# Feed-forward with seven block products in every second pair, two weight block sums made by accumulating transfers

## What is computed

```python
def sq_relu_mlp(h, w1, w2):
    return jnp.square(jax.nn.relu(h @ w1)) @ w2

x = x + g2 * sq_relu_mlp(h2, w1[l], w2[l])   # h2: 256 x 2048, w1: 2048 x 8192, w2: 8192 x 2048
return rmsnorm(x, final_norm_g)
```

## Time and profile before

| | |
|---|---|
| median of 3 runs | 1491.27 us (1491.06 to 1492.92) |
| profiled execution | 1491.33 us, of which the span from first to last instruction is 1489.5 |
| TensorE busy | 1459.4 us (98%), 7252 matmuls; granted clock 0.998 |
| VectorE busy | 1107.0 us (74%) |
| ScalarE busy | 710.5 us (48%) |
| GpSimd busy | 115.0 us (8%) |
| transfers | 355.95 MB, mean 239 GB/s |

### The profile page before, as it was taken

The page is one execution under the profiler, slowest core; times in us unless marked ns, Lnnn a source line. Parts: engine busy times, 40 slices in busy tenths (PEclk is TensorE's granted clock), DMA queues, the critical chain, the costliest instruction groups (busy, mean ns, idle before and its releaser), DMA issues.

```text
span 1489.5 us, 18858 instructions
## 1 busy us (share of the span) xinstructions
PE 1459.4 (98%) x7252; PEld 1201.0 (81%) x7252; DVE 1107.0 (74%) x1342; ACT 710.5 (48%) x996; POOL 115.0 (8%) x92
## 2 busy tenths in 40 slices
PE   5999999999999999999999999999999999999997
PEld 2567888888888888888888888888888888888886
DVE  2456866867667678998777568778757999789976
ACT  3423444565554453334454434434444666456654
POOL 0000000101000000010100000000301322002200
PEclk9999999999999999999999999999999999999999
DMA  9997776764666679889665577787575665656552
GB/s 368 379 361 261 261 253 210 225 201 144 233 216 229 224 226 356 322 295 356 242 223 155 163 264 273 262 306 268 191 235 177 202 216 187 195 183 222 194 197 81
DMA packets 123053, 355.95 MB, mean 239 GB/s; under 512 B 10962, under 2 KB 11986, under 8 KB 122322
## 3 DMA queue, kind: packets, MB, share of 16 engines
q1 hardware_dynamic: 121348, 353.17, 69.7%
q10 hardware_dynamic: 1616, 1.57, 0.3%
HBM read 352.60 MB, written 2.10 MB: 238 GB/s over the span
## 4 chain that ended last, share of the span: by engine, by line
PE 88%; DVE 5%; ACT 2%; issue 2%; DMA 2%; ACTq 0%; POOL 0%; POOLq 0%; DVEq 0%
PE bank L1691 20%; PE bank L1693 20%; PE bank L1692 20%; PE bank L1977 14%; PE bank L1980 7%; PE bank L1847 2%; DVE wl L1202 2%; PE bank L1820 1%; DMA raw<-in_w_ada 1%; ACT wh L748 1%; PE bank L1722 1%; PE bank L1810 1%; DVE acc L1233 1%; DMA ident<-in_identity 1%; PE bank L1773 0%
## 5 line engine op out<-in xcount | busy, mean ns | idle before, releaser
L1202 DVE TENSOR_TENSOR wl<-raw,wh 128x1024 fp32r<-128x1024 f32 x425 | 527.5, 1257 | 227.6 <-ACT wh L748 209.2
L748 ACT ACTIVATE wh<-raw 128x1024 fp32r<-128x1024 f32 x328 | 341.5, 1059 | 296.8 <-PE bank L1980 141.5
L1977 PE MATMUL bank<-h2S,wh 128*128 128x512 f32 x896 | 245.2, 395 | 0.8 <-DVE wl L1202 0.7
L1691 PE MATMUL bank<-wh,hT 128*128 128x512 f32 x512 | 206.8, 404 | 0.5 <-DVE wl L1202 0.5
L1693 PE MATMUL bank<-wh,hT 128*128 128x512 f32 x512 | 200.1, 391 | 0.0
L1692 PE MATMUL bank<-wl,hT 128*128 128x512 f32 x512 | 199.7, 390 | 0.0
L1977 PEld LDWEIGHTS bank<-h2S,wh 128*128 128x128 f32 x896 | 153.1, 189 | 21.9 <-DVE wl L1202 0.9
L1024 ACT ACTIVATE wh<-raw 128x1024 fp32r<-128x1024 f32 (+1 forms) x128 | 125.8, 1002 | 70.3 <-PE bank L1693 64.2
L1233 DVE SCALAR_TENSOR_TENSOR acc<-raw,cc,acc 128x1024 f32<-128x1024 f32 x120 | 153.5, 1279 | 0.0
L1691 PE MATMUL bank<-wh,hidS 128*128 128x512 f32 x392 | 152.6, 389 | 0.3 <-DVE wl L1202 0.3
L1980 PEld LDWEIGHTS bank<-h2S,wl 128*128 128x128 f32 x896 | 137.5, 189 | 19.0
(11 more groups left out here) (253 smaller groups left out, 2075.9 us busy)
## 6 DMA issues: line engine op xcount, KB each, us to landing
raw<-in_w SPq DMA_DIRECT2D x256, 512.0 KB, 4.7
raw<-in_w_ada SPq DMA_DIRECT2D x192, 512.0 KB, 6.0
raw<-in_w_in SPq DMA_DIRECT2D x128, 512.0 KB, 4.6
raw<-in_w_attn_o SPq DMA_DIRECT2D x32, 512.0 KB, 6.4
raw<-in_w_out SPq DMA_DIRECT2D x32, 512.0 KB, 5.8
raw<-in_w_fourier SPq DMA_DIRECT2D x16, 512.0 KB, 6.8
xt<-in_x SPq DMA_DIRECT2D x2, 1024.0 KB, 6.4
ct<-in_ctx SPq DMA_DIRECT2D x2, 1024.0 KB, 11.0
```

The lines of the kernel that those rows point to most:

```text
L748: nc.scalar.activation(slot, raw[:, s % RAW, :], ACT.Copy).then_inc(wh_done, 1)
L1202: nc.vector.tensor_tensor(lo, raw[:, s % RAW, :], hi.bitcast(F32), ALU.subtract)\
L1691: nc.tensor.matmul(bank[b][:], a_hi, w_hi, start=first, stop=False)
L1977: nc.tensor.matmul(out[:], wh[:, slot, cols_f[f]], h2S[:, block, :, :].rearrange("p v t -> p (v t)"), start=(block == 0), stop=False)
```

## The change

Sevens stand in every second pair: 4, 6, ..., 26 of the first block (12) and 5, 7, ..., 25 of the second (11), 23 in place of 15. Two of the four weight sums are no longer made by DVE. SP loads the upper right block of the pair twice into a buffer `tS` (two of them, in turn), and GpSimd issues two transfers that add the upper left and the lower right block to it on the way (accumulating transfers); DVE makes the two other sums, both behind the plain pair. ACT copies the halves of `tH` before the token parts, and `tH` may be overwritten once TensorE's fifth product of the seven before has used it (`t_used`). The combination runs in a buffer `comb` of its own place (over `tL`) and begins two pairs behind the last seven, with its last two steps together.

```diff
-SEVEN_AT = ((3, 6, 9, 12, 15, 18, 21, 24), (5, 8, 11, 14, 17, 20, 23))
+SEVEN_AT = ((4, 6, 8, 10, 12, 14, 16, 18, 20, 22, 24, 26), (5, 7, 9, 11, 13, 15, 17, 19, 21, 23, 25))
...
-COMBINE_AT = {3: ("first", "second"), 4: (0,), 5: (1,), 6: (2,), 7: (3,)}
+COMBINE_AT = {2: ("first", "second"), 3: (0,), 4: (1,), 5: (2, 3)}
...
-PRESCALED_AT = {6: 0, 9: 1, 12: 2, 15: 3}
+PRESCALED_AT = {6: 0, 8: 1, 9: 2, 11: 3}
...
-        tF = place("tF", [P, 4, HC], F32, "h")
+        tF = place("tF", [P, 2, HC], F32, "h", 4096)
...
+        comb = place("comb", [P, 4, HC], F32, "h", 16384)
+        tS = [place("tS0", [P, 2, HC], F32, "h"), place("tS1", [P, 2, HC], F32, "f", 4096)]
...
                 sp.dma_start(raw[:, (S2 + n) % RAW, :], w2[k * P:(k + 1) * P, col * NC:(col + 1) * NC]).then_inc(raw_full[(S2 + n) % RAW], 16)
+                if n % 2 == 0 and n // 2 + 1 in SEVENS[1:]:
+                    i = n // 2 + 1
+                    s = SEVENS.index(i)
+                    c, p = divmod(i, NP)
+                    if s == 1:
+                        sp.wait_ge(hid_ready, 4 + 2 * (N1 - 1))
+                    if s >= 2:
+                        sp.wait_ge(t_lo, 2 * s - 2)
+                        sp.wait_ge(t_sum, s - 1)
+                    for j in range(2):
+                        sp.dma_start(tS[s % 2][:, j, :], w2[2 * p * P:(2 * p + 1) * P, c * NC + HC:(c + 1) * NC]).then_inc(t_first[s % 2], 16)
...
-            for i in SEVENS:
-                _, p, s, _ = PAIRS[i]
-                k1, k2 = 2 * p, 2 * p + 1
+            def token_sums(s):
+                k1, k2 = 2 * PAIRS[SEVENS[s]][1], 2 * PAIRS[SEVENS[s]][1] + 1
                 if s:
                     pool.wait_ge(a_lo, 3 * s)
...
+            def weight_sums(s):
+                c, p, _, _ = PAIRS[SEVENS[s]]
+                row, col = 2 * p * P, c * NC
+                if s == 0:
+                    pool.wait_ge(t_start, 32)
+                else:
+                    pool.wait_ge(t_first[s % 2], 32 * (s // 2 + s % 2))
+                nc.gpsimd.dma_start(tS[s % 2][:, 0, :], w2[row:row + P, col:col + HC], accum_op=ALU.add).then_inc(t_acc[s % 2], 16)
+                nc.gpsimd.dma_start(tS[s % 2][:, 1, :], w2[row + P:row + 2 * P, col + HC:col + NC], accum_op=ALU.add).then_inc(t_acc[s % 2], 16)
+
+            pool.wait_ge(gemm_done, M2)
+            p = SEVENS[0]
+            for j in range(2):
+                nc.gpsimd.dma_start(tS[0][:, j, :], w2[2 * p * P:(2 * p + 1) * P, HC:NC]).then_inc(t_start, 16)
+            pool.wait_ge(hid_ready, 4 + 2 * (N1 - 1))
+            token_sums(0)
+            weight_sums(0)
+            for s in range(1, len(SEVENS)):
+                weight_sums(s)
+                token_sums(s)
...
             def seven_hi(i, p, s):
+                if s:
+                    act.wait_ge(t_used, s)
+                act.wait_ge(t_acc[s % 2], 32 * (s // 2 + 1))
+                nc.scalar.activation(tH[:, 0:2, :], tS[s % 2][:], ACT.Copy).then_inc(t_hi, 1)
+                act.wait_ge(t_sum, s + 1)
+                nc.scalar.activation(tH[:, 2:4, :], tF[:], ACT.Copy).then_inc(t_hi, 1)
+                tile_hi(2 * i, HC)
                 if s == 0:
                     act.wait_ge(row_done, 4)
...
-                for j in range(2):
-                    act.wait_ge(t_sum, 2 * s + j + 1)
-                    nc.scalar.activation(tH[:, 2 * j:2 * j + 2, :], tF[:, 2 * j:2 * j + 2, :], ACT.Copy).then_inc(t_hi, 1)
-                tile_hi(2 * i, HC)
                 tile_hi(2 * i + 1)
...
-                    if following is not None:
-                        block_sums(i + 1, following, e)
...
+                if following is not None:
+                    block_sums(i + 1, following)
+
+            def block_sums(i, s):
+                n2 = 2 * i + 1
+                r2 = raw[:, (S2 + n2) % RAW, :]
+                dve.wait_ge(raw_full[(S2 + n2) % RAW], 16 * ((S2 + n2) // RAW + 1))
+                dve.wait_ge(t_acc[s % 2], 32 * (s // 2 + 1))
+                if s:
+                    dve.wait_ge(t_lo, 2 * s)
+                then(nc.vector.tensor_tensor(tF[:, 0, :], tS[s % 2][:, 0, :], r2[:, HC:NC], ALU.add))
+                nc.vector.tensor_tensor(tF[:, 1, :], tF[:, 0, :], r2[:, 0:HC], ALU.add).then_inc(t_sum, 1)
...
-                direct(1, 6, tH[:, 3, :], tL[:, 3, :])
+                direct(1, 6, tH[:, 3, :], tL[:, 3, :]).then_inc(t_used, 1)
```

## The result

The changed kernel takes 1499.79 us (median, 1499.40 to 1500.33), beside 1491.16 us for the kernel before on the same chip: a ratio of 1.0056, with a 95% interval of 1.0041 to 1.0071. It is slower by more than the 0.2% that can be told. The forecast was 1492.4 with a range of 1486.5 to 1501: the range held the time, but the forecast is 7.4 us too low, and the time lies outside the 1490 to 1495 that it gave itself as its own range.

What follows compares the result with a forecast made beforehand. TensorE was taken as the bound by 1.06 us per three pairs, VectorE after the change. From 1491.33 us, less 5.8, plus 6.8 for VectorE and the tail, plus 0.1 for a restart: 1492.4 us, range 1486.5 to 1501.

Steps and rivals of the forecast that it cites:

- TensorE's saving, 5.8 us: TensorE, whole stage: 24 matmuls fewer save 5.44 us, and the first seven's 0.36 us lateness goes; together 5.8 us.
- VectorE's 10.50 for two pairs: VectorE between sevens: one plain pair and one seven take 10.50 us against TensorE's 10.20, later by 0.30 us.
- The lead of 1.1 us and what is lost behind it: VectorE starts each block 1.1 us ahead; TensorE then loses 2.2 us in the first block, 4.3 in the second.
- Tail, 0.3 us: Behind pair 30: one combination step more, 1.4 us, mostly taken up by idle time; 0.3 us is added.
- The chain of fill and accumulation in the steady state, nothing: Fill, two accumulations and two sums between sevens: 14.3 to 22.8 us of 21.0 available; low half taken, costing nothing.
- rival 2: Fill-and-accumulate chain ends last at ACT's and VectorE's wait for the sums; halfway costs 8.5 us, 1501 us; chance 0.14.
- The first accumulation leaves when the first token sums end: Stage start, GpSimd: first accumulation leaves about 1150, needed some 6 us later; 0 to 1 us, taken as 0.
- The clock: TensorE after a wait: only 0.1 us was added to the forecast for a restart.
- VectorE packs tighter: VectorE between sevens packs a little tighter than 10.50 us, so TensorE stays the bound: 1487.1 us; chance 0.18.
- the transfers don't relieve it: VectorE waits as long as the sums took: 1.20 us back in 21 intervals, 25 us, 1517 us; chance 0.04.
- GpSimd's issues slow it: GpSimd's issue of accumulations slows VectorE, in the middle 0.33 us x 21: 7 us, 1499.4 us; chance 0.12.
- the forecast's own range: The forecast case itself, 1490 to 1495 us from 0.1 us either way in an interval; chance 0.52.

Runs made afterwards that it cites:

- the run with later fills: Changed kernel with a small early GpSimd addition, first accumulations ahead of the token sums, and the second seven's fills one pair later on SP: 1494.28 us, ratio 1.0020.
- the run with the small addition: Changed kernel plus one 128x1 GpSimd addition directly behind its second row sum, order of the stage unchanged: 1498.80 us, ratio 1.0047.
- both edits: Changed kernel with the 128x1 GpSimd addition behind the last row sum and the first seven's accumulations issued ahead of its token sums: 1495.21 us, ratio 1.0026.

## Why the prediction was right or wrong, by its steps

- **TensorE's saving, 5.8 us.** Right: 24 fewer matmuls, and the pitch of 0.2267 holds.
- **VectorE's 10.50 for two pairs.** Right to 0.01 us, from the packed rows and a subtraction. The run with four sums (11.82) shows the 1.32 that the transfers take, where the working had 1.20; the run without sums shows that nothing else binds behind the start.
- **The lead of 1.1 us and what is lost behind it.** First block: 1.7 us measured (0.21, then five times 0.3), 2.2 forecast. This is no clean confirmation, since the late start gave VectorE time to get ahead. Where the first seven is nearly on time (the run with later fills) the block loses 3.7 us, eleven times 0.3 and 0.4 for one late landing: the lead isn't there, because VectorE waits for the first sums and not for ACT alone. Second block: 4.0 measured, 4.3 forecast, with the prescaled products' intervals at 11.11 and 11.09, 0.6 over 10.5 as priced.
- **Tail, 0.3 us.** Right: the last gap between matmul starts is 1480.36 - 1479.33 = 1.03, and was 0.69.
- **The chain of fill and accumulation in the steady state, nothing.** Right for the changed kernel's profiled execution, but with less margin than the 6 us of the working. Median landings of 4.7 and 6.9 us lie in its bounds of 4.8 and 8.2 (the fill 0.1 below), and no interval behind the second seven is longer than VectorE's own work makes it. But single landings reach 9.6 us, and ACT waited for sums four times, once at the start and three times later:
```profile
ACT tH L1073 <- DMA tS<-in_w: 16.1, 4, 7.5
```
  In three other runs such a landing came too late for VectorE and lengthened one interval: by 0.4 us with later fills (10.91), 0.5 with the accumulations first (11.01), 0.9 with the small addition (11.38). So rival 2 is at work now and then, not in every interval.
- **"The first accumulation leaves when the first token sums end, about 1150, and is needed some 6 us later: 0 to 1 us, taken as 0."** This step failed, and it cost 5.0 us in place of 0. The first accumulation left 2.9 us later, for the delay of the first tensor instruction behind the all-reduce, which the fills had brought out from under the wait for `hid`. And the sums came 8.8 us after the second had left, which is beyond even the working's upper bound of 8.2; in the run with the small addition it was 10. The landing is the larger part: with the delay gone the first seven was still 3.5 us late. That other transfers had a share in it, the run with later fills shows (1.6 us). The step took the stage's median landing for its first, and asked what the fills cost the queues but not what they were put ahead of on GpSimd.
- **The clock.** The forecast priced a wait of TensorE at its own length. Behind this one came 2.95 us more.

Counted up in the profiled execution: 5.0 + 2.95 more, 0.5 and 0.3 less in the two blocks, is 7.2 us of the 1499.87 - 1492.4 = 7.5 that are missing. A cross-check is the run with later fills, where the start is nearly mended: 0.7 late, 3.7 and 4.15 in the blocks, 0.34 in the tail are 8.9, against the 6.9 of the forecast, which makes 1494.4; its profiled execution took 1494.48.

**The rivals.** That VectorE packs tighter is refuted by 10.50, that the transfers don't relieve it by 11.82, that GpSimd's issues slow it by the unchanged 10.50; so the 1499.4 of that rival, the number nearest to the time, is a coincidence. The fill-and-accumulate chain as the bound was put at 1501, also near, but for another reason: in the changed kernel it ends last once, at the start, and not 0.45 us in each of 19 intervals. The upper end of the range came from these two rivals. That it held the time is luck: without them the forecast's own range, to 1495, would have missed it.

With the start nearly mended, 23 sevens still take 1494.3 us. The change loses because a seven in every second pair leaves no gap in which VectorE can catch up: the last two of the eight new sevens bring 6 matmuls, 1.4 us, and TensorE's losses inside the blocks go from 0.26 us (21 sevens, the first at pair 5) to 7.9 (23). The best version leaves these two out and lets TensorE set the pace.

## What to carry to other kernels

When an instruction is put ahead of others on an engine's queue, ask what cost of a first instruction, seen in no row of its own, the ones behind it carry, and what wait used to hide it; a tiny instruction of the same kind, issued in the idle stretch before, takes it out of the way. The first instance of a repeated step needs its own sum: its landing time is that of the burst in which it starts, not the median. And where two engines lie within 3%, add work of the new kind only as far as the slower one's slack goes, then leave a gap.

## What the runs showed of the hardware that was not expected

- GpSimd's first tensor instruction behind a partition all-reduce comes after 7.82 to 8.56 us of "issue" where it stands by itself (six runs), and after 7.80, 9.70, 10.43, 11.87 and 12.23 where transfers have been issued in between (the changed kernel and the four runs without the early addition that issue transfers); later ones behind a transfer's issue follow at once. Why the transfers lengthen it is open.
- GpSimd's issue of a transfer can block for want of descriptor memory, as it seems until earlier ones have landed: 44 stalls, 169 us, with half of it.
- An accumulating transfer of 256 KB landed in 4.0 to 9.6 us in the changed kernel (up to 11.7 with both edits), median 6.9 over 1160 to 1270, a fill of the same size in 4.7. The Trainium skill (DMA: Bandwidth & Descriptors, Anatomy of one DMA) fits 2.0 us plus the bytes over 436,000 for GpSimd's transfers, 2.6 us for this size; by that the first sums would have been there at about 1156. The rows, with the DMA engines nearly full beside it (a share of 0.95 from 1155 to 1160, 1.00 from 1186 to 1207), show none under 4.0 us, and they decide.
- TensorE's granted clock fell to half behind each of its idle times from 2.34 us up: 4.86 in the changed kernel, 4.59, 3.33, 3.18, 2.80 and 2.50 in other runs, eleven from 2.34 to 5.15 with half the descriptor memory. It fell behind none up to 1.68 us. In between it fell behind 1.88 and 1.98 (four sums) and 1.95 (half the descriptor memory), and not behind 2.21 (both edits), so the length of the idle time alone doesn't decide it. Behind 1.88 and 2.50 it fell only about 1 us after TensorE had started again. In the changed kernel the lower level held for some 6 us and 14 matmuls, behind 3.18 (21 sevens) and 2.80 for some 3 us.
- One token addition of GpSimd, 0.8 to 0.9 us elsewhere, took 5.45 us, and VectorE's operations beside it had their short durations (two `wl` in 1.82 us, where they take 2.09 beside other token sums):
```profile
1353.46 5.45 POOL L719 TENSOR_TENSOR aF<-hid 128x128 f32<-128x128 f32 x1 [4.64 <-DVE aL L1619]
...
1353.30 1.82 DVE L1622 TENSOR_TENSOR wl<-raw,wh 128x512 fp32r<-128x512 f32 x2
```
So here, as the rows read, GpSimd was held off and VectorE wasn't. It isn't the transfers: the run with four sums has none, and a token addition of 6.05 us near the same place. What decides between the two no run here tests.
